# A two-layer attention and RWKV backbone on one core: softmax probabilities divided on GpSimd before their transposes, and modulation rows picked by transposes and a sum

## The reference, cut to what matters

```python
def attend(q, k, v, scale):
    ...
    s = jnp.einsum('bqkgd,blkd->bkgql', qg, k).astype(jnp.float32) * scale
    p = jax.nn.softmax(s, axis=-1).astype(v.dtype)
    o = jnp.einsum('bkgql,blkd->bqkgd', p, v)
...
mod_x = jnp.split((s_c @ ada_w + ada_b)[:, None, :], ADALN_CHUNKS, axis=-1)
mod_c = jnp.split((s_cc @ ada_w + ada_b)[None, None, :], ADALN_CHUNKS, axis=-1)
```

## Time and profile before

| | |
|---|---|
| time, median of 3 runs | 2668.17 us (2666.22 to 2672.42) |
| the profiled execution's own time | 2663.25 us |
| its span | 2661.4 us |
| attention stage in it | 195.5 to 476.7 us |
| busy: PE, DVE, ACT, POOL | 2376.8, 1103.5, 959.5, 580.2 us |
| mean granted TensorE clock | 0.957 of full |

### The profile page before, as it was taken

How to read it: one execution, slowest core, us unless ns; L and a number is a source line. 1 busy time by engine, 2 the same in 40 slices (tenths; PEclk the granted TensorE clock), 3 DMA queues, 4 the chain that set the end, 5 groups by cost and what they waited for, 6 DMA issues and landing times.

```text
span 2661.4 us, 65202 instructions
## 1 busy us (share of the span) xinstructions
PE 2376.8 (89%) x27599; PEld 1966.4 (74%) x27599; DVE 1103.5 (41%) x2324; ACT 959.5 (36%) x1614; POOL 580.2 (22%) x367
## 2 busy tenths in 40 slices
PE   5989999989999999599957889989898976899998
PEld 4767777878888888488736777777777765688886
DVE  2335655341111112441364666766766643311112
ACT  3555555342121212322343443444344322422323
POOL 0320000223232322122222112111121102344442
PEclk9999999989999999799988999999999977899999
DMA  7124544111111111022410000000000002222221
GB/s 234 48 64 150 168 159 143 48 48 64 63 63 63 63 63 63 32 83 84 131 43 21 11 14 22 11 14 22 11 14 22 4 2 79 79 95 95 95 94 63
DMA packets 172537, 176.09 MB, mean 66 GB/s; under 512 B 26496, under 2 KB 160016, under 8 KB 172304
## 3 DMA queue, kind: packets, MB, share of 16 engines
q1 hardware_dynamic: 172304, 172.62, 20.6%
HBM read 161.06 MB, written 11.53 MB: 65 GB/s over the span
## 4 chain that ended last, share of the span: by engine, by line
PE 81%; DVE 10%; issue 4%; ACT 3%; DMA 1%; SPq 1%; POOL 0%; ACTq 0%; DVEq 0%; PEldq 0%
PE PS L375 45%; PE PS L1154 4%; PE PS L395 3%; PE PS L603 2%; PE PS L1139 2%; PE PS L1254 2%; PE PS L630 2%; PE PS L962 2%; PE PS L1134 2%; PE PS L582 1%; PE PS L1246 1%; PE PS L612 1%; PE PS L1234 1%; DVE SMS L737 1%; PE PS L896 1%
## 5 line engine op out<-in xcount | busy, mean ns | idle before, releaser
L355 POOL TENSOR_TENSOR WL<-RAW,WH 128x1024 fp32r<-128x1024 f32 x184 | 439.7, 2412 | 1341.0 <-ACT WH L349 1341.0
L375 PE MATMUL PS<-AH,WH 128*128 128x512 f32 (+1 forms) x1320 | 474.3, 359 | 84.8 <-DVE AL L820 38.8
L375 PE MATMUL PS<-AH,WL 128*128 128x512 f32 (+1 forms) x1320 | 472.7, 358 | 0.0
L375 PE MATMUL PS<-AL,WH 128*128 128x512 f32 (+1 forms) x1320 | 469.1, 355 | 0.0
L375 PEld LDWEIGHTS PS<-AH,WH 128*128 128x128 f32 x1320 | 253.4, 192 | 133.8 <-issue 54.8
L349 ACT ACTIVATE WH<-RAW 128x1024 fp32r<-128x1024 f32 x184 | 183.8, 1047 | 267.2 <-PE PS L375 265.5
L375 PEld LDWEIGHTS PS<-AL,WH 128*128 128x128 f32 x1320 | 251.9, 191 | 37.2
L375 PEld LDWEIGHTS PS<-AH,WL 128*128 128x128 f32 x1320 | 253.2, 192 | 33.7
L375 PE MATMUL PS<-BH,WL 128*128 128x512 f32 (+1 forms) x768 | 273.4, 356 | 0.0
L375 PE MATMUL PS<-BH,WH 128*128 128x512 f32 (+1 forms) x768 | 272.6, 355 | 0.0
L375 PE MATMUL PS<-BL,WH 128*128 128x512 f32 (+1 forms) x768 | 271.5, 353 | 0.0
(11 more groups left out here) (233 smaller groups left out, 4097.5 us busy)
## 6 DMA issues: line engine op xcount, KB each, us to landing
ADW<-l_ada_w SPq DMA_DIRECT2D x40, 1024.0 KB, 5.2
RAW<-l_mlp_up SPq DMA_DIRECT2D x64, 512.0 KB, 4.4
RAW<-l_mlp_down SPq DMA_DIRECT2D x64, 512.0 KB, 4.0
RAW<-l_w_rkv SPq DMA_DIRECT2D x24, 512.0 KB, 4.6
rwkv_scratch<-STG SPq DMA_DIRECT2D x24, 384.0 KB, 2.6
ADA<-l_ada_w SPq DMA_DIRECT2D x4, 2048.0 KB, 17.0
RAW<-l_w_in SPq DMA_DIRECT2D x16, 256.0 KB, 5.7
RAW<-l_w_out SPq DMA_DIRECT2D x16, 256.0 KB, 5.2
```

The lines of the kernel that those rows point to most:

```text
L355: e.tensor_tensor(WL[:, s, rows], RAW[:, s, rows], WH[:, s, rows], ALU.subtract).then_inc(w_split[h], 1)
L375: mm = e.matmul(dst, w[:, s, k, n * P:(n + 1) * P], r[:, k, lo:hi], start=(k == 0 and i == 0), stop=(k == KT - 1 and i == 2), skip_group_c ...
```

## The change

The reciprocals are no longer spread. POOL gets a program for the attention: for each pair it waits for the reciprocals and multiplies PB in place, head 0 then head 1, by the reciprocal column broadcast along the row (128 x 768 elements in a full pair, 128 x 256 in a short one). PE's transposes wait for these products (`p_scaled`) in place of the exps. `spread`, RB and its ACT copy are gone, and the OT step is a plain copy of bank 7.

The pick of modulation rows is no longer two products with SEL but two transposes of the 128 x 128 halves of EV into 256 columns of bank 3; DVE sums four columns each into PK (128 x 2 x 2) and then adds the bias.

```diff
             def transposes(m):
                 for i in parts(m):
-                    e.wait_ge(e_done, 2 * m + 1 + max(j for j, _, _ in blocks(m, i)))
+                    e.wait_ge(p_scaled, 2 * m + 1 + max(j for j, _, _ in blocks(m, i)))
...
-            def spread(m):
-                e.wait_ge(r_done, m + 1)
-                for j in range(2):
-                    rs = 24 + 2 * (m % 4) + j
-                    mm = e.matmul(bank(3)[64 * j:64 * j + 64, 260:260 + P], SMS[:, rs:rs + 1].to_broadcast([P, HD]), IDN,
-                                  start=True, stop=True, skip_group_check=True)
-                mm.then_inc(rb_done, 1)
...
                 if 1 <= k <= PAIRS:
                     e.wait_ge(e_done, 2 * k)
-                    e.wait_ge(rb_ready, k - 1)
                     e.wait_ge(ada_read, chunks_before(PICK_AT, k))
                 if k in PICK_AT:
                     n = PICK_AT[k]
                     e.wait_ge(ev_ready, n + 1)
                     for h in range(2):
-                        e.matmul(bank(3)[:, 256 + 2 * h:258 + 2 * h], EV[:, n % 2, h * P:(h + 1) * P], SEL,
-                                 start=True, stop=True, skip_group_check=True)
-                if 1 <= k <= PAIRS:
-                    spread(k - 1)
+                        e.transpose(bank(3)[:, 256 + P * h:256 + P * h + P], EV[:, n % 2, h * P:(h + 1) * P], IDN)
...
-                    e.wait_ge(rb_done, k)
-                    if k >= 3:
-                        e.wait_ge(o_done, k - 2)
-                    e.activation(RB[:, k % 2, :], bank(3)[:, 260:260 + P], ACT.Copy).then_inc(rb_ready, 1)
                     evac(k - 1, 2)
...
+        def attn_pool(e):
+            for m in range(PAIRS):
+                e.wait_ge(r_done, m + 1)
+                for j in range(2):
+                    p = PB[:, m % 2, j, 0:span(m) * P]
+                    rs = 24 + 2 * (m % 4) + j
+                    e.tensor_tensor(p, p, SMS[:, rs:rs + 1].to_broadcast([P, span(m) * P]), ALU.mult).then_inc(p_scaled, 1)
...
                     e.wait_ge(e_done, 2 * k)
                     s = 2 * ((k - 1) % 4)
+                    if k >= 5:
+                        e.wait_ge(p_scaled, 2 * (k - 4))
                     e.reciprocal(SMS[:, 24 + s:26 + s], SMS[:, 16 + s:18 + s]).then_inc(r_done, 1)
...
                     e.wait_ge(pv_done, k - 1)
-                    e.wait_ge(rb_ready, k - 1)
                     e.wait_ge(q_low, 2 * mg + 2)
-                    e.tensor_tensor(OT[:, mg, mr * P:(mr + 1) * P], bank(7)[:, 0:P], RB[:, (k - 1) % 2, :],
-                                    ALU.mult).then_inc(o_done, 1)
+                    e.tensor_copy(OT[:, mg, mr * P:(mr + 1) * P], bank(7)[:, 0:P]).then_inc(o_done, 1)
...
                     e.wait_ge(s_done, 2 * k + 2)
-                    e.tensor_tensor(MOD[:, :, :, :].rearrange("p l c v -> p (l c) v")[:, 2 * n + 16:2 * n + 18, :],
-                                    bank(3)[:, 256:260].rearrange("p (n v) -> p n v", v=2),
+                    e.tensor_reduce(PK[:, :, :], bank(3)[:, 256:512].rearrange("p (n j w) -> p n w j", n=2, j=4)[:, :, 0:2, :],
+                                    AX.X, ALU.add).then_inc(pick_sum, 1)
+                    e.wait_ge(pick_sum, n + 1)
+                    e.tensor_tensor(MOD[:, :, :, :].rearrange("p l c v -> p (l c) v")[:, 2 * n + 16:2 * n + 18, :], PK[:, :, :],
                                     PAR[:, 2 * n + 16:2 * n + 18].unsqueeze(2).to_broadcast([P, 2, 2]),
                                     ALU.add).then_inc(ada_read, 1)
...
-            with pool.Fori(U_OUT0 // 2, U_OUT1 // 2) as i:
+            pool_split(pool, U_OUT0, 0)
+            attn_pool(pool)
+            pool_split(pool, U_OUT0 + 1, 1)
+            with pool.Fori(U_OUT0 // 2 + 1, U_OUT1 // 2) as i:
```

More of the change, by code:

```diff
@@ L184, in build @@
         KL2 = [place(f"KL2{p}", 30 + 12 * p, [P, 2, T], F32R) for p in range(2)]
+        PK = place("PK", 112.25, [P, 2, 2])
         EV = place("EV", 108, [P, 2, UC])
@@ L188, in build @@
         SMS = place("SMS", 112, [P, 32])
-        RB = place("RB", 112.25, [P, 2, P])
         BH = place("BH", 48, [P, KT, T], F32R)
@@ L290, in build @@
         pv_done, o_done = sem("pv"), sem("o_scaled")
-        rb_done, rb_ready = sem("recip_spread"), sem("recip_copied")
+        p_scaled, pick_sum = sem("probs_scaled"), sem("pick_sum")
         ot_high, ot_low = sem("ot_high"), sem("ot_low")
```

## The result

| | before | changed |
|---|---|---|
| time, median | 2667.19 us (4 runs) | 2697.16 us (2692.58 to 2700.97, 4 runs) |
| the profiled execution: span | 2661.4 us | 2698.5 us |
| its attention stage | 281.2 us | 306.8 us (197.9 to 504.7) |
| the 47 intervals between reciprocals | 268.75 us | 293.46 us |

The ratio of the changed kernel to the one before is 1.0109 with a 95% interval of 1.0095 to 1.0122: slower by 1.1%. The forecast was 2716 us, between 2698 and 2738. The profiled execution of the changed kernel was the longest of its four, and the one of before (2663.25 us) was shorter than any of its four, so the two spans lie 37.1 us apart, not 30.

The account below looks back on a forecast made before the run. PE's work bounded a full pair before; the change would close a series loop through POOL. Intervals 310 against 268.75 us (+41.3), last pair +1.5, clock +5: +48 in all, median 2716 us, range 2698 to 2738.

Parts of the forecast that it names:

- The loop: Layer 0 attention: reciprocal to reciprocal all in series through POOL, PE and DVE; 7.94, 6.95 or 5.34 us per interval.
- the term POOL: POOL's two products per pair in attention: 1.81 us for 768 columns, 3.61 us a full pair, 1.45 a short one.
- Nothing in the trace has a broadcast operand on POOL: On pricing POOL's product: no such row seen, so 1.81 us taken from other two-input rows, between 0.74 and 2.5.
- The rival of a short product: POOL's product near 0.74 us, PE bounds, about 2640 us; no difference at some 1.2 us per 768 columns; chance 0.06.
- the clock: PE's clock falls to 1.2 GHz in three of eight intervals behind a short pair (r = 2), 1.6 us each: +5 us.
- The tail: Last pair of the attention, from its reciprocal to OT: 6.6 us before, +1.5 with POOL in it.
- The other stages keep their code, so I take their time as unchanged: Stages outside layer 0's attention: no change in time; later stages of the same length.
- The clock rival: PE at half speed behind all 32 full pairs, 51 us on top, about 2762 us; in half, 2737; chance 0.14.
- Contention: DVE's wide subtractions (L673) and POOL block one another: up to 19 us, 2735; chance 0.15 together with a slower product.
- DVE's extra sum of the pick adds an instruction and a wait on itself, under 0.4 us: Ahead of head 1's row maximum in DVE's queue; hidden, otherwise up to 0.4 x 40 = 16 us.
- The cover named for it: Head 1's row maximum feeds an exp that waits longer for ACT's copy of part 0, hiding DVE's extra sum.
- the removed 0.6 us per pair pays nothing: PE's saving on pick and spread, 29 us in all if PE bounds, only makes PE idle longer while POOL works.

Follow-up runs that it names:

- Run 2: Changed kernel with POOL multiplying only the first half of each head's columns, the rest left undivided; 2648.1 us, ratio 0.9929 to the kernel before.
- run 3: Changed kernel with the reciprocal of pair k-1 moved ahead of the row maximum of (k, 0) in DVE's queue; 2644.3 us, ratio 0.9919.
- Run 1: Changed kernel with POOL multiplying by a stored full-width tile instead of the broadcast reciprocals, so probabilities are not divided; 2731.0 us.
- run 6: Changed kernel with the old pick (two selector products, one DVE addition from PSUM), reciprocal still behind the row maximum; 2696.7 us, ratio 1.0132.
- run 5: Kernel before, with the reciprocal of pair k-1 moved ahead of the row maximum of (k, 0) in DVE's queue; 2655.9 us, ratio 0.9974.
- run 8: Changed kernel with the reciprocal first and one reciprocal per head, POOL waiting for each head's own; 2640.9 us, ratio 0.9923.

## Why the prediction was wrong in size

**The loop was right.** The prediction named the series reciprocal, POOL, transposes, modulation product, scores, row maximum, reciprocal, and its price as the longer of loop and PE's work. The steps measured are 0.24 (0.23 in the prediction), 0.06 (0.07), 1.02 (0.97), 1.00 (1.00), 2.08 or 1.08 (2.06, 1.07). Run 2 shows that full intervals follow POOL's time one for one, run 3 that they stop doing so when the reciprocal leaves its place behind the row maximum.

**The failed step is the term POOL.** "So 768 columns should take 1.264 + 256 x 2.1 ns = 1.81 us; a full pair takes 3.61 us, a short one 1.45." A product with a broadcast operand took 1.45 us, 2.89 a full pair and 1.18 a short one. Over 31 full and 16 short pairs that is 31 x 0.72 + 16 x 0.27 = 27 us too much. The prediction bounded the product by 0.74 and 2.5 us, but chose the line of the rows nearest in kind and left the range no room for what lies between: its low end was set by 1.6 us. Run 1 puts a full operand back, and the predicted number appears.

The sentence "Nothing in the trace has a broadcast operand on POOL" is also wrong. L1121, one of the three points of the line, has one:

```python
e.tensor_tensor(lta(b, 4 * i), lta(b, 4 * i),
                table("eye64").unsqueeze(1).to_broadcast([P, 4, C]), ALU.add).then_inc(lta_ready, 1)
```

It repeats a block of 64 columns four times, and it took 726 ns, as much as the 727 ns of a stored tile in run 1. One column repeated along the row took 613 ns for the same 256 columns. So "broadcast" alone does not tell the price. What part the form of the repeat has in it is not isolated: L1121 is an addition, and its first operand lies in blocks too.

The rival of a short product had the direction of this error right, but the product was not short enough to change the sign. Its break-even of some 1.2 us is a little high: on a straight line between run 2 (0.83 us, 17.7 us below before) and the changed kernel (1.47 us, 30 us above) no difference would come at about 1.07 us, an estimate. The figure from the page "GPSIMD Engine Reference" of the Trainium skill, section "Elementwise — side-by-side cycle accounting", about 2.6 cycles an element for `tensor_tensor`, gives 1.66 us at the 1.2 GHz of its example, an estimate (the prediction has 1.72). It is nearer but still above the measured 1.47, and for two full operands it is below the 1.81 of run 1.

**The rest of the sum.** The forecast for the intervals was 41.3 us, and the product takes 27 off it; measured were 24.7, some 10 more than what is left. Of these 6 are the clock, for which I had 5 in a term of its own: the intervals behind a short pair at 250.8, 362.2 and 474.3 us took 8.2, 8.8 and 8.9 us in place of 7.3, and the first 7.1 in place of 5.1. Another 2.7 are the steps that were 0.05 to 0.07 us longer than forecast in each of 40 intervals, and 1.2 come from the seven intervals without a modulation product, which were shorter by 5.8 us in all and not by 7. In the first of the three slow intervals, PE stood 1.86 us for POOL and then had transposes at half the rate:

```profile
252.60 1.11 PE L612 MATMUL PS<-CK,PB 128*128 128x128 f32 x4 [1.86 <-POOL PB L723]
254.02 1.97 PE L612 MATMUL PS<-CK,PB 128*128 128x128 f32 x8 [0.31 <-POOL PB L723]
```

That is 1.2 GHz again (0.72 granted on average from 252 to 258). Three such intervals of eight is what was forecast. The place was argued, but the count was picked and not worked out: that it came out is luck. And the reading behind it was off: the prediction has PE standing from 243.05 to 245.57 in the kernel before, but the pick (L655) runs there from 243.72 to 244.30, so there were two gaps, of 0.67 and 1.28 us, and not one of 2.5. The tail took 7.6 us instead of 6.6, with +1.5 forecast.

"The other stages keep their code, so I take their time as unchanged" put a second term at nothing. In the profiled executions they are 11.5 us longer in the changed kernel: 2.4 us ahead of the attention, and some nine in the recurrence of layer 1, where the same instructions run 29.5 us late against the kernel before at 1582 us and 38.5 us late at 2039. Over the same stretch runs 3 and 6 lose nine and seven us against the kernel before, and run 5 five. Why is open; no run was made on it. The stage alone gives 25.6 us of the 37.1 between the profiled executions.

So it is in part luck that the time lies only 0.8 us outside the range. With the measured products in the prediction's own sum, the median would have been 2716 - 27 = 2689 us, 8 us too low.

**The other rivals.** The clock rival (32 falls) did not come. Contention was real but elsewhere than I had it: not in L661 (L673 before), which took 0.97 us on average against 0.95, but in the addition of the picked rows, off the loop. The step "DVE's extra sum of the pick adds an instruction and a wait on itself, under 0.4 us" missed that the edit turned an addition with one input in SBUF into one with two. The cover named for it held: run 6 removes it, and nothing changes. That "the removed 0.6 us per pair pays nothing" is right for the changed kernel, by run 6 for the pick; that it pays once the loop is open, runs 3 and 5 show together: with the reciprocal first in both, the changed kernel is ahead.

## What to carry to other kernels

When a step is moved to an idle engine, follow the wait it creates through every in-order queue until it comes back to its start; here the time of the idle engine decided the sign only because a reciprocal stood behind a row maximum that needed the result of the previous round. Before such a change is given up, look for the one instruction whose place in a queue closes the loop. And an operand form that no row shows should keep the range open down to the next form below, not only to a small discount on the nearest row. Whether a row shows it is read from the code of its line: the profile's row gives the shape of the result, not how an operand is repeated.

## What was not expected of the hardware

A GpSimd product of two full float32 operands takes 727 ns for 256 columns and 1812 ns for 768, 2.1 ns a column; with the second operand one column broadcast along the row 613 and 1467 ns, 1.7 ns a column (826 ns for 384). A second operand that repeats a block of 64 columns four times was as dear as a full one: 726 ns for 256 columns (L1121, an addition).

A DVE addition of 128x4 elements took 161 to 1483 ns in the changed kernel, where both inputs are in SBUF, and 162 ns on average in run 6, where one input is in PSUM. In both, 34 of the 40 additions met a GpSimd product. In run 6 none was held up. In the changed kernel 25 were, and took 0.37 to 1.48 us; the other 15, which met no product or fell where one product ended and the next began, took 0.16 to 0.17. The changed kernel's row, then run 6's:

```profile
L761 DVE TENSOR_TENSOR MOD<-PK,PAR x40: 161/941/1483, 214.4 to 491.6; 128x4 f32<-128x4 f32 x40
```

```profile
L759 DVE TENSOR_TENSOR MOD<-PS,PAR 128x4 f32<-128x4 f32 x40 | 6.5, 162 | 27.2 <-PE PS L603 27.2
```

In the interval shown above it started at 379.97, as POOL's second product did, and ended at 381.45, 0.02 us after that product's end at 381.43. All that were held up ended some 0.02 us behind the end of a product. Against the 0.16 us of an addition that meets no product, nearly all of the 1.48 us is waiting. The rule of the Trainium skill's page "SBUF — State Buffer", section "Who interferes with whom", that a DVE instruction with two SBUF inputs contends with a GpSimd one that reads SBUF, was weighed in the prediction for the wide subtractions only; the trace agrees with it for an instruction on four columns. The holding is mutual. In run 8:

```profile
301.70 0.95 DVE L661 TENSOR_TENSOR QS<-QKV,QS 64x768 fp32r<-64x768 f32 x1
301.75 2.24 POOL L723 TENSOR_TENSOR PB<-PB,SMS 128x768 f32<-128x768 f32 x1 [2.57 <-DVE SMS L745]
...
302.69 2.11 DVE L669 TENSOR_TENSOR KL<-QKV,KH 64x768 fp32r<-64x768 f32 x1
```

The subtraction that was first took its usual 0.95 us, and the product 0.05 us behind it 2.24 in place of 1.47. The next subtraction started inside the product and took 2.11 us in place of 0.95.
